# Expert blocks of 32 rows in four column tiles, with the second product of a block issued behind the first product of the next

## What is computed

```python
def grouped_moe(u, w_router, w1, w3, w2):
    xt = u.reshape(B * T, D)                       # T = 512 tokens, D = 1024
    aff = softmax(xt @ w_router)                   # 16 experts in 4 groups
    ...                                            # best group, top 2 experts inside it
    gate = ...                                     # two weights per token, 0 elsewhere
    for e in range(N_EXPERTS):                     # 16
        h = silu(xt @ w1[e]) * (xt @ w3[e])        # D_EXPERT = 512
        y = y + gate[:, e:e + 1] * (h @ w2[e])
```

## Time and profile before

| | us |
|---|---|
| median of 3 runs | 908.73 |
| lowest and highest | 901.06 and 910.23 |
| the profiled execution | 904.57 |
| its span, first to last instruction | 902.9 |
| PE busy in the span | 756.2 |
| the weights' queue (q1), share of 16 transfer engines | 47.8% |

### The profile page before, as it was taken

How to read it: one execution, slowest core, us unless ns; L and a number is a source line. 1 busy time by engine, 2 the same in 40 slices (tenths; PEclk the granted TensorE clock), 3 DMA queues, 4 the chain that set the end, 5 groups by cost and what they waited for, 6 DMA issues and landing times.

```text
span 902.9 us, 11766 instructions
## 1 busy us (share of the span) xinstructions
PE 756.2 (84%) x4258; PEld 459.0 (51%) x4259; DVE 314.5 (35%) x742; ACT 236.8 (26%) x609; POOL 79.6 (9%) x148
## 2 busy tenths in 40 slices
PE   0599999787999999777799931999999999999970
PEld 0544555544675665566544631555555555555530
DVE  3634355221547556455323440112121211211114
ACT  2011001042334444344302201222332223323220
POOL 5010000151000000000000011000000000000013
PEclk9689999868589999979699855999999999999995
DMA  8784623512990000000090447199999999998217
GB/s 319 284 335 186 233 102 131 160 36 75 335 237 30 0 0 0 1 1 0 9 363 0 162 165 256 38 369 373 379 383 375 374 373 378 386 374 309 46 46 279
DMA packets 74488, 178.42 MB, mean 198 GB/s; under 512 B 5014, under 2 KB 19934, under 8 KB 71390
## 3 DMA queue, kind: packets, MB, share of 16 engines
q1 hardware_dynamic: 65328, 152.90, 47.8%
q0 software_dynamic: 4736, 14.95, 4.7%
q10 hardware_dynamic: 4400, 10.25, 3.7%
HBM read 156.33 MB, written 21.76 MB: 197 GB/s over the span
## 4 chain that ended last, share of the span: by engine, by line
PE 79%; DVE 7%; DMA 4%; ACT 4%; issue 3%; POOL 2%; SPq 0%; POOLq 0%; ACTq 0%; DVEq 0%
PE score L1523 20%; PE bank L1214 13%; PE score L1535 10%; PE score L1445 6%; PE bank L1312 5%; PE score L1333 4%; PE bank L1304 3%; PE bank L1516 2%; PE bank L1388 2%; DVE pool_sb L792 2%; PE bank L1257 2%; PE bank L1529 1%; PE score L1485 1%; ACT pool_sb L550 1%; PE bank L1377 1%
## 5 line engine op out<-in xcount | busy, mean ns | idle before, releaser
L1523 PE MATMUL score<-pool_sb,featT 128*64 128x256 f32 x1600 | 185.9, 385 | 5.6 <-issue 3.2
L1523 PEld LDWEIGHTS score<-pool_sb,featT 128*64 128x64 f32 x1600 | 123.1, 138 | 68.5 <-issue 24.1
L1214 PE MATMUL bank<-pool_sb,featT 128*128 128x512 f32 (+2 forms) x320 | 115.1, 523 | 2.9 <-DVE pool_sb L819 1.9
L1535 PE MATMUL score<-pool_sb,featT 128*64 128x512 f32 x400 | 96.9, 605 | 0.0
L1214 PEld LDWEIGHTS bank<-pool_sb,featT 128*128 128x128 f32 x320 | 61.9, 194 | 55.8 <-issue 49.9
L1153 DVE TENSOR_TENSOR featT<-featT,score 128x128 f32<-128x128 f32 x50 | 14.4, 287 | 177.5 <-ACT featT L645 177.5
L792 DVE SCALAR_TENSOR_TENSOR pool_sb<-pool_sb,cond 128x2048 f32<-128x2048 f32 x24 | 56.3, 2348 | 2.0 <-DMA pool_sb<-in_ada_w 0.6
L1445 PE MATMUL score<-pool_sb,featT 128*128 128x512 f32 x128 | 56.7, 603 | 0.0
L1146 DVE TENSOR_SCALAR featT<-bank,mod_col 128x64 f32<-128x64 f32 x104 | 28.6, 336 | 80.1 <-PE bank L1516 80.1
L757 POOL DMA_DIRECT2D expert_rows<-featT x50 | 26.2, 524 | 304.7 <-DVE featT L1158 303.0
L550 ACT ACTIVATE pool_sb<-score,nmax 128x128 f32<-128x128 f32 (+3 forms) x64 | 33.1, 522 | 69.7 <-PE bank L1304 60.7
(11 more groups left out here) (257 smaller groups left out, 828.8 us busy)
## 6 DMA issues: line engine op xcount, KB each, us to landing
pool_sb<-in_moe_w SPq DMA_DIRECT2D x48, 2048.0 KB, 19.8
pool_sb<-in_ada_w SPq DMA_DIRECT2D x24, 1024.0 KB, 5.4
expert_rows<-zeros_f SPq DMA_DIRECT2D x17, 512.0 KB, 6.4
featT<-expert_rows ACTq DMA_DIRECT2D x27, 256.0 KB, 6.4
expert_rows<-featT POOLq DMA_DIRECT2D x50, 128.0 KB, 5.7
pool_sb<-in_w_in SPq DMA_DIRECT2D x2, 2048.0 KB, 9.3
pool_sb<-in_w_out SPq DMA_DIRECT2D x4, 1024.0 KB, 16.6
x_sb<-in_x SPq DMA_DIRECT2D x1, 2048.0 KB, 9.3
```

The lines of the kernel that those rows point to most:

```text
L1214: m = nc.tensor.matmul(banks[4 + i][:, 0:n], featT[:, k, i * P:(i + 1) * P], w_stage[:, g % 3, k, 0:n], start=(k == 0), stop=(k == KD - 1))
L1523: mm = nc.tensor.matmul(banks[s][h * BT:(h + 1) * BT, 0:2 * P], xgT[:, k, :], w13[:, :, k, at0:at0 + P], start=(k == 0), stop=(k == KD - 1))
L1535: mm = nc.tensor.matmul(banks[2][h * BT:(h + 1) * BT, :], hT[:, s, c * BT:(c + 1) * BT], w2[:, 2 * c + s, h * 512:(h + 1) * 512], start=(s ...
```

## The change

Blocks become 32 rows, the array is split in four column tiles of 32 columns, and every expert has at least two blocks. With the counts above the blocks are 3, 2, 3, 2, 2, 3, 2, 3, 3, 2, 2, 3, 3, 4, 3, 2, which makes 42.

- `inner` computes all hidden columns in one step: 8 pieces k times 4 tiles, 32 products of 256 streamed columns. `outer` is 16 products of 256 columns.
- `stage_of` sets PE's order: `inner(g)`, the 8 transposes of the next rows together (`next_rows`), `outer(g - 1)`, and the transpose of the hidden rows of block g, now one. Before, `outer(g)` stood in the block's own iteration.
- ACT and DVE do one silu, one product and one readout of the hidden rows per block. ACT's load of the rows of g + 2 stands before the readout of the hidden rows instead of behind it.
- DVE's `rows_out(g)` follows the work of block g + 1. POOL stores the result with four transfers of 32 rows and 256 columns instead of two of 64 rows and 512.
- PE's `outer(g)` also waits for `m_ye`, since DVE now reads `outer`'s PSUM bank one block later.
- SP's waits count one `m_h1` per block instead of two.

```diff
-BT = 64
-MAXB = (2 * T) // BT + NE - 1
+BT = 32
+NT = P // BT
+HB, DN = DE // NT, D // NT
+MIN_BLOCKS = 2
+MAXB = (2 * T) // BT + MIN_BLOCKS * NE
...
-                sp.wait_ge(m_h1, hi * 2)
+                sp.wait_ge(m_h1, hi)
...
+            def block_of_rows(g):
+                act.wait_ge(m_h1, g + 1)
+                nc.scalar.activation(silu, banks[0][:, 0:HB], ACT.Silu).then_inc(m_si, 1)
+                xg_T(g + 1)
+                act.wait_ge(m_xt_v, g + 2)
+                xg_load(g + 2)
+                act.wait_ge(m_ht, g + 1)
+                nc.scalar.activation(hT, banks[6][:, 0:P], ACT.Copy).then_inc(m_hT, 1)
...
             with act.Fori(0, total) as g:
-                silu_half(g, 0)
-                hT_half(g, 0)
-                silu_half(g, 1)
-                xg_T(g + 1)
-                hT_half(g, 1)
-                act.wait_ge(m_xt_v, g + 2)
-                xg_load(g + 2)
+                block_of_rows(g)
...
-            with pool.Fori(0, total) as g:
-                pool.wait_ge(m_ye, g + 1)
-                for h in range(2):
-                    pool.dma_start(xs[bass.ds(g * BT, BT), h * 512:(h + 1) * 512], y_sb[h * BT:(h + 1) * BT, :]).then_inc(s_ys, 16)
+            def store_rows(y, g):
+                pool.wait_ge(m_ye, g + 2)
+                for h in range(NT):
+                    pool.dma_start(xs[bass.ds(g * BT, BT), h * DN:(h + 1) * DN], y[h * BT:(h + 1) * BT, :]).then_inc(s_ys, 16)
...
-            ch(nc.vector.tensor_scalar(nb, tot, 1.0, 1.0 / BT, ALU.max, ALU.mult))
+            ch(nc.vector.tensor_scalar(nb, tot, (MIN_BLOCKS - 1) * BT + 1.0, 1.0 / BT, ALU.max, ALU.mult))
...
+            def rows_out(y, g, stored):
+                dve.wait_ge(m_y, g + 1)
+                if stored:
+                    dve.wait_ge(s_ys, g * (16 * NT))
+                nc.vector.tensor_tensor(y, banks[2][:, 0:DN], gate2_part[:], ALU.mult).then_inc(m_ye, 1)
+
+            def block_of_rows(g):
+                dve.wait_ge(m_si, g + 1)
+                nc.vector.tensor_tensor(hmid, silu, banks[0][:, HB:2 * HB], ALU.mult).then_inc(m_h, 1)
                 xg_T(g + 1)
...
+            with dve.Fori(1, total - 1) as g:
+                block_of_rows(g + 1)
+                rows_out(y_sb, g, True)
+            rows_out(y_last, total - 1, False)
...
+            def inner(slot, g):
+                pe.wait_ge(m_xa, g + 1)
+                pe.wait_ge(m_xv, g + 1)
+                for k in range(KD):
+                    if k == KD - 1:
+                        pe.wait_ge(s_xg, g * 16 + 32)
+                    for h in range(NT):
+                        mm = nc.tensor.matmul(banks[0][h * BT:(h + 1) * BT, 0:2 * HB], xgT[:, k, :], exp_w13[slot][:, :, k, h * HB:(h + 1) * HB],
                                               start=(k == 0), stop=(k == KD - 1))
...
+            def outer(g, slot):
+                pe.wait_ge(m_hT, g + 1)
+                pe.wait_ge(m_ye, g + 1)
+                for c in range(NT):
+                    for h in range(NT):
+                        mm = nc.tensor.matmul(banks[2][h * BT:(h + 1) * BT, 0:DN], hT[:, c * BT:(c + 1) * BT],
+                                              exp_w2[slot][:, c, h * DN:(h + 1) * DN], start=(c == 0), stop=(c == NT - 1))
...
+            def stage_of(g, slot, slot_before, uses):
+                pe.wait_ge(e_w13[slot], uses * 32)
+                inner(slot, g)
+                next_rows()
+                pe.wait_ge(e_w2[slot], uses * 16)
+                outer(g - 1, slot_before)
+                inner_T(g)
+
+            def expert(e, slot, uses):
+                lo, hi = blocks_of(pe, e)
+                stage_of(lo, slot, (slot + 2) % 3, uses)
+                with pe.Fori(lo + 1, hi) as g:
+                    stage_of(g, slot, slot, uses)
```

More of the change, by code:

```diff
@@ L1517, in xg_T @@
                 m.then_inc(done, 1)
-            def inner(w13, s, ks):
-                for k in ks:
-                    for h in range(2):
-                        at0 = h * HB + s * P
-                        mm = nc.tensor.matmul(banks[s][h * BT:(h + 1) * BT, 0:2 * P], xgT[:, k, :], w13[:, :, k, at0:at0 + P],
-                                              start=(k == 0), stop=(k == KD - 1))
-                return mm
-            def hT_half(g, s):
-                pe.wait_ge(m_h, g * 2 + (s + 1))
-                nc.tensor.transpose(banks[6 + s][:, 0:P], hmid[:, s, :], ident[:]).then_inc(m_ht, 1)
@@ L1561, in _ @@
             xg_T(0, m_xt_v)
+            pe.wait_ge(e_w13[0], 32)
+            inner(0, 0)
+            next_rows()
+            inner_T(0)
             pe.wait_ge(t_gs, 1)
+            with pe.Fori(1, blocks_of(pe, 0)[1]) as g:
+                stage_of(g, 0, 0, 1)
             with pe.Fori(0, NE // 3) as n:
-                for b in range(3):
-                    expert(n * 3 + b, b, n)
-            expert(NE - 1, 0, NE // 3)
+                for j in range(3):
+                    expert(n * 3 + (j + 1), (j + 1) % 3, n + (1 + j // 2))
+            outer(all_blocks(pe) - 1, 0)
 _INS = ['x', 'c', 'w_router', 'ada_w', 'ada_b', 'norm1_g', 'norm2_g', 'w_in', 'w_out', 'nsa_q_gain', 'nsa_k_gain',
```

89 lines of the change are left out of this document (32 added, 57 removed).

## The result

| | before | after |
|---|---|---|
| median of 20 runs, us | 906.97 | 914.05 |
| lowest and highest | 899.83 and 910.23 | 905.82 and 921.81 |
| ratio after / before, 95% interval | | 1.0066, 1.0040 to 1.0092 |
| the profiled execution and its span | 904.57, 902.9 | 918.79, 917.1 |
| PE busy in the span | 756.2 | 738.2 |

A forecast was written before the change was run, and what follows sets the result against it. PE bounded the kernel before; afterwards transfer loops set 8.2 us per block under the weight stream. 579.6 + 242 + 60.8 = 882.4, PE's end 887.4, span 915.8, so 918 us was forecast, range 880 to 942.

The forecast's parts named there:

- the likeliest case: Blocks under the weight stream: a pace between 7.7 and 8.7 us, own range 905 to 929 us; chance 0.46.
- the sum: Stage of the experts: start, blocks under and behind the stream, and end added to a span of 915.8 us, up 1.4%.
- PE's cost per block: PE's work for 32 rows: first product 3.6, second 1.87, transposes 0.7, hidden transpose 0.26, together 6.4 us.
- The rival with two abreast: PE's column tiles: four don't run abreast, a block costs 11.9 us, span some 1077 us; chance 0.04.
- Loop B: Results: DVE's readout, POOL's four issues, landing of the stores, DVE again; 8.2 us per block, from 5.2 to 8.7.
- The rival by which small transfers come back soon: Landings under the stream fall with the bytes, PE sets 6.4 us a block, span 862.6 us, 4.5% faster; chance 0.25.
- Loop A: Rows: PE's transposes, ACT's reading and load issue, landing, PE's last 8 records; 8.1 us per block, from 5.9 to 9.0.
- PE's wait ahead of the last piece: PE idle ahead of `inner`'s last piece, released by the row load, some 1.8 us in each of about 30 blocks.
- The stream: Weight loads of the loop: 242 us at 371 GB/s, in which 29.5 blocks pass at 8.2 us.
- The clock: PE's clock falls as it idles: up to 0.7 us per block, span 930 us; chance as main cause 0.08.
- Costed at nothing: Silu, product and readout on ACT and DVE, small copies and a memset, weight waits, SP's order: no cost.

The follow-up runs named there:

- one store of four: Changed kernel, but POOL stores only the first of the four column tiles of each block's result; ratio 0.9752 to the kernel before, span 875.2 us.
- two buffers: Changed kernel with a second result buffer, even and odd blocks each having a buffer and a semaphore; ratio 0.9715 to the kernel before, span 881.5 us.
- the late wait: Changed kernel with PE's wait for the next rows moved behind `inner`, directly ahead of the transposes; alone, ratio 1.0022 to the kernel before, span 911.8 us.
- the best version: Changed kernel with both a second result buffer and PE's wait for rows moved behind `inner`; ratio 0.970 to the kernel before, span 875.5 us.
- the single larger store: One 128 KB store per block instead of four, on the changed kernel with two buffers and the late wait; ratio 0.980 to the kernel before, span 883.4 us.

## Why the prediction held, step by step

Forecast and median are 918 and 914 us. The mechanism of the likeliest case, a pace between 7.7 and 8.7 us under the stream set by a loop through a transfer, is what the traces show, with a pace of 7.9. Between the two profiled executions the change is 1.6% (904.57 to 918.79), near the 1.4% of the sum. Between the medians it is 0.8%, and the ratio of the first table is 0.66%, since the execution profiled of before lies 0.3% under its median of 20 runs and that of after 0.5% over its own. So the change counts as under 1%, which had 0.29, and not as slower, which had 0.46. By the medians the 12.9 us of the sum are 7.1. That the sum comes within 1.3 us of the profiled span is in part luck: this execution is the second longest of the 20, and the errors of its parts, below, nearly cancel.

Two readings in the prediction are off. Its own sum puts the span 1% below before at a pace of 7.35 us, with landings of 4.85 and 4.45, and not at 7.6, which gives 901. And of the six slices of the earlier trace rows at seven tenths busy it names four; the other two show eight tenths of clock. Neither changes the forecast.

**The account.** The sum gave a span of 915.8; the profiled span is 917.1. The places where the sum can be read, the start, SP's last issues in the loop, and the end, one fence each:

```profile
561.44 6.30 PE L1538 MATMUL score<-pool_sb,featT 128*32 128x256 f32 x64 [1.15 <-DVE featT L1151]
...
570.41 5.25 PE L1538 MATMUL score<-pool_sb,featT 128*32 128x256 f32 x64 [1.62 <-issue]
...
582.04 1.00 SPq L421 DMA_DIRECT2D pool_sb<-in_moe_w  x2
```

```profile
784.96 47.63 SPq L421 DMA_DIRECT2D pool_sb<-in_moe_w  x7
```

```profile
877.18 0.68 PE L1528 MATMUL bank<-ident,featT 32*128 32x32 f32 x8
...
883.50 0.68 PE L1528 MATMUL bank<-ident,featT 32*128 32x32 f32 x8
...
886.77 1.93 PE L1551 MATMUL score<-pool_sb,featT 128*32 128x256 f32 x32 [0.47 <-DVE featT L1159]
...
893.40 0.20 POOL L762 TENSOR_TENSOR pool_sb<-pool_sb 128x4 f32<-128x4 f32 x1 [1.28 <-DMA expert_rows<-featT]
```

| step | predicted | measured |
|---|---|---|
| SP starts the loop's stream | 579.6 | 582.0 |
| blocks under the stream | 29.5 at 8.2 = 242 | 33 at 7.93 = 261.7 |
| blocks behind it | 9.5 at 6.4 = 60.8 | 6 at 6.64 = 39.8 |
| last `inner` done | 882.4 | 883.5 |
| PE ends | 887.4 | 888.7 |
| POOL's first step behind the stores | 892.8 | 893.4 |
| span | 915.8 | 917.1 |

The parts add up: +2.3 at the start, -1.2 in the 39 blocks, +0.2 to PE's end, -0.7 to POOL's step and +0.7 behind it, +1.3 together.

**PE's cost per block: right.** Predicted 6.4, measured 6.32 (877.18 to 883.50; of the last six distances three are 6.32, two 6.55 and 6.65, and the first, with the stream's end in it, 7.68). Four column tiles run abreast: 64 records of 256 columns in 3.59 us, 56 ns each. The rival with two abreast is out. The rule of about 62 ns per matmul where the sequencer decodes in microcode (the Trainium skill, TensorE: Matmul & The Clock Gate, Wait — 56ns, not 53.3ns?) would give an estimate of 4.0 us for these 64 records; the rows do not show it.

**Loop B: right in its mechanism, 0.3 us too long.** By the terms of the sum: readout 0.42 (0.42), to POOL 0.66 (0.65), three more issues 1.74 (1.77), landing 4.9 to 5.1 (5.3), DVE's start 0.03 (0.05): 7.8 us against 8.2. That is the common case. Of the 30 landings in the chain of 583 to 843 us, 15 take 4.8 to 5.2 us and 12 take 5.4 to 7.7, which is why the mean pace is 7.9 though the first four distances are near 7. The landing did not fall to the 1.8 of an idle queue, nor stay at 5.8. The rival by which small transfers come back soon failed here: 3.4 us of surcharge on 32 KB, against 3.5 on 128 KB before.

**Loop A: mis-sized.** I let ACT issue the load behind its four readouts, 1.85 us behind the transposes' start. The timeline has the transposes at 652.92 and the issue at 653.76, 0.84 later, while two readouts are still to come: their records go on to 654.57. With a landing of 5.4 (predicted 5.6) and 0.57 for PE (589.66 to 590.23; predicted 0.65), the loop is 6.8 and not 8.1. The versions in which it binds run at this pace: 6.83 with one store of four, 6.79 with two buffers. PE's wait ahead of the last piece, foretold with 1.8 us in each of about 30 blocks, came in 17, with 19.6 us together. Since I had both loops near 8.1 and the longer one counts, the sum did not suffer; with a shorter loop B it would have.

**The stream: a wrong assumption, covered by another.** I took its 242 us as given and asked how many blocks pass in it. It took 261, at 347 GB/s. The last matrix is issued behind the last `outer` of expert 12, and experts 0 to 12 have 33 blocks, whatever the pace; the stream starts with the third of them, and the last `outer` stands one block late, so that 31 blocks pass up to that issue and two more up to the landing. SP's issues end at 784.96 + 47.63 = 832.6, and it lands at 843. A matrix lands 12.3 us after its issue, where it took 22.0 before: SP now issues with fewer matrices in the queue, which fits its waiting for slots. So PE's pace stretches the stream as much as the stream stretches the landing; 33 slow blocks and not 29.5 (+5.4 us), each 0.27 shorter (-8.0), and six behind at 6.64 (+1.4). With two buffers the same stream ends at some 827 and with the late wait too at some 823.

**The clock: seen, but without a price here.** The rival said that idle PE would lose its clock. It did: the granted clock is 0.95 in 583 to 843, where it was 1.00 before, and in the two-buffer version, where PE idles less, it is 1.00 again (245 us, PE busy 233). In the timeline `outer` takes 3.41 us at 645.73 and 3.08 at 661.78 instead of 1.93. Yet the readouts of these blocks stand 7.78 and 7.79 us from the next: the slow records lie in time in which PE would have waited for the stores. A price of its own it had only at the start of the stage: `inner(1)` took 5.25 us instead of 3.66, which with 0.8 of other delay make the +2.3 us there. In the profiled execution with one store of four the first two products took 4.97 and 3.66 us instead of 6.30 and 5.25. What the falls would cost where nothing covers them was not tried.

**Costed at nothing: right, but for a term that was not named.** Among PE's waits from 560 us on none is for weights, for ACT's silu or for its readout of the hidden rows beyond 0.6 us. The missing term: PE starts late at the start of some experts' loops, released by nothing that the trace shows, 7.3 us in 15 places from 560 us on (1.6 of them ahead of `inner(1)`), where it was 3.2 in 7 before. In the version with two buffers and the late wait one wait for weights of 4.1 us appears: its cover, the slow pace, is gone.

**What stays open.** Why some landings take 7 us and others 5; whether the late wait gains its 0.1 us per block with one buffer; what part of the 12 us between the best version (875.5) and the run without a stream (863.7) is the one stall at 738 us (7 us by its distance); and why the single larger store costs 8 us where nobody waits for it (PE's waits for weights are 3.3 us longer there). The new order on blocks of 64 rows, without column tiles of 32, was not tried.

## What to carry to other kernels

When a block gets half as long, list each loop that closes through a transfer issued once per block, and add up its whole length with the landing as it is under the load of that stage: a buffer that exists once is a loop, and here it ran at 7.8 us under work of 6.3. Such a bound hides the worth of other edits, so the order of PE's work should be judged again after the second buffer is in, and the second buffer with the new order. When a weight stream waits for slots, the number of blocks that pass beside it follows from the slots and not from its bandwidth.

## What the runs showed of the hardware

- A saturated stream of 2 MB loads adds about the same, at the median, to each small transfer: 3.4 us to a store of 32 KB and 3.2 us to a load of 128 KB, where it added 3.5 and 3.1 to four and two times the bytes in the kernel before.
- Stores from POOL's queue of 32 pieces of 1 KB, 64 of 2 KB and 128 of 1 KB land in 1.7, 2.3 and 4.2 us when no weights move; the last two have the same bytes, but 48 and 144 packets. One issue of 128 pieces (0.69 us on POOL) is no quicker home than four of 32 pieces (2.24 us on POOL).
- ACT issues a transfer before the readouts that stand ahead of it in its program have ended: 653.76 for readouts that end at 654.57.
- `inner` of a new expert can start 0.5 to 0.8 us late, released by nothing that the trace shows: 0.53 at 585.24 and 0.83 at 639.43 in the changed kernel, 0.56 at 657.90 with two buffers and the order undone.
- With idle gaps of 1 to 3 us per block the granted clock fell to the lower level at times: 0.95 on average in 583 to 843 us with PE at 87%, and 1.00 in the two-buffer version with PE at 95%. With the order undone and one buffer it was 0.99 over the same 260 us with PE at 84%, its wait in most blocks being the 0.8 us for ACT.
